# An encoder trunk with three attention kinds: values as the stationary operand in column halves, gates and gated outputs feature-major

## The reference

```python
def encoder_layer(x, ...):
    h = x @ w_in                                   # 2912 columns
    (a_q, a_k, a_v, a_g, b_cq, b_ckv, b_kr, b_g, c_q, c_k, c_v, c_g) = split(h)
    oa = window_attn(a_q, a_k, a_v, sink, t5_bias) * silu(a_g)   # 8 heads, 2 key heads, +-128 tokens
    ob = mla(b_cq, b_ckv, b_kr, ...) * silu(b_g)                 # 4 heads, all positions, rotary part
    oc = neighborhood_attn(c_q, c_k, c_v, rpb) * silu(c_g)       # 4 heads, 8x16 window of a 64-wide grid
    o = concatenate([oa, ob, oc]) @ w_out          # 512 + 256 + 256 rows
    return layer_norm(alpha * x + o)
```

## Time and profile before

| | |
|---|---|
| median of 3 runs | 2085.67 us (2085.27 to 2086.95) |
| the profiled execution, first to last instruction | 2085.9 us |
| outside that span | the span is as long as the runs' time, so nothing to add |
| mean granted TensorE clock | 0.979 of full speed |
| PE busy | 1942.8 us (93%) in 13746 instructions |
| PEld busy | 1712.9 us (82%) |
| DVE, ACT, POOL busy | 950.3 (46%), 815.9 (39%), 440.2 us (21%) |
| waits of DVE for products (line 990, 1147, 1001) | 160.0, 142.1, 68.3 us |
| first layer: input, A, C, prologue, B, output of the long sequence | 386 to 640, to 727, to 776, to 815, to 948, to 1054 us |

### The profile page before, as it was taken

The page is one execution under the profiler, slowest core; times in us unless marked ns, Lnnn a source line. Parts: engine busy times, 40 slices in busy tenths (PEclk is TensorE's granted clock), DMA queues, the critical chain, the costliest instruction groups (busy, mean ns, idle before and its releaser), DMA issues.

```text
span 2085.9 us, 35268 instructions
## 1 busy us (share of the span) xinstructions
PE 1942.8 (93%) x13746; PEld 1712.9 (82%) x13746; DVE 950.3 (46%) x2266; ACT 815.9 (39%) x1883; POOL 440.2 (21%) x476
## 2 busy tenths in 40 slices
PE   1899999999999999999959999989999999999996
PEld 0699778789998875999948986888899977689896
DVE  7335654511245655444442455452124366544436
ACT  3334652412225565443123356341231365644412
POOL 4322311410020152001132213122101114400013
PEclk9999999999999999999979999999999999999998
DMA  6455314321127010005044460422212341000312
GB/s 250 128 195 159 74 48 145 101 61 41 41 77 177 12 47 1 1 1 176 28 129 153 141 165 12 156 77 81 61 41 64 105 107 58 1 1 1 122 62 82
DMA packets 143083, 176.23 MB, mean 84 GB/s; under 512 B 18576, under 2 KB 128784, under 8 KB 142400
## 3 DMA queue, kind: packets, MB, share of 16 engines
q1 hardware_dynamic: 140976, 167.54, 26.2%
q10 hardware_dynamic: 1504, 4.78, 0.6%
q0 software_dynamic: 432, 1.57, 0.2%
HBM read 148.63 MB, written 35.80 MB: 88 GB/s over the span
## 4 chain that ended last, share of the span: by engine, by line
PE 88%; DVE 5%; ACT 3%; issue 1%; DMA 1%; POOL 1%; SPq 0%; ACTq 0%; DVEq 0%; POOLq 0%
PE psum L528 59%; PE psum L651 14%; PE psum L625 8%; PE psum L600 5%; DVE x_lo L981 2%; PE psum L538 1%; DVE hT L931 1%; ACT pAC L782 1%; DMA qkC<-ln_in_b 0%; DVE qB_lo L1123 0%; POOL w_lo L421 0%; PE psum L607 0%; PE psum L510 0%; ACT qB_hi L889 0%; ACT w_hi L814 0%
## 5 line engine op out<-in xcount | busy, mean ns | idle before, releaser
L528 PE MATMUL psum<-w_hi,x_hi 128*128 128x256 f32 x2112 | 594.5, 281 | 12.0 <-issue 7.7
L528 PE MATMUL psum<-w_lo,x_hi 128*128 128x256 f32 x2112 | 591.9, 280 | 0.0
L528 PE MATMUL psum<-w_hi,x_lo 128*128 128x256 f32 x2112 | 591.5, 280 | 0.0
L528 PEld LDWEIGHTS psum<-w_hi,x_hi 128*128 128x128 f32 x2112 | 399.2, 189 | 13.3 <-issue 13.2
L528 PEld LDWEIGHTS psum<-w_hi,x_lo 128*128 128x128 f32 x2112 | 399.0, 189 | 0.0
L528 PEld LDWEIGHTS psum<-w_lo,x_hi 128*128 128x128 f32 x2112 | 398.0, 188 | 0.2
L421 POOL TENSOR_TENSOR w_lo<-w_stage,w_hi 128x1024 fp32r<-128x1024 f32 (+1 forms) x74 | 156.7, 2123 | 743.3 <-ACT w_hi L814 743.3
L421 DVE TENSOR_TENSOR w_lo<-w_stage,w_hi 128x1024 fp32r<-128x1024 f32 (+1 forms) x70 | 140.3, 2014 | 283.4 <-ACT w_hi L814 283.4
L814 ACT ACTIVATE w_hi<-w_stage 128x1024 fp32r<-128x1024 f32 (+1 forms) x144 | 127.6, 938 | 236.1 <-PE psum L528 209.7
L790 ACT ACTIVATE pt_sb<-psum 128x256 f32<-128x256 f32 (+2 forms) x224 | 113.2, 505 | 258.8 <-PE psum L625 258.2
L1207 POOL TENSOR_TENSOR hT<-hT,rinv 128x256 f32<-128x256 f32 x96 | 58.8, 612 | 686.0 <-DVE rinv L1022 686.0
(11 more groups left out here) (140 smaller groups left out, 2925.6 us busy)
## 6 DMA issues: line engine op xcount, KB each, us to landing
w_stage<-w_in SPq DMA_DIRECT2D x72, 512.0 KB, 4.5
w_stage<-w_out SPq DMA_DIRECT2D x32, 512.0 KB, 3.9
toep<-rpb_tile SPq DMA_DIRECT2D x12, 1152.0 KB, 13.2
hT<-y SPq DMA_DIRECT2D x24, 512.0 KB, 4.7
y<-hT SPq DMA_DIRECT2D x24, 512.0 KB, 2.6
w_stage<-w_in SPq DMA_DIRECT2D x40, 256.0 KB, 3.3
rpb_tile<-rpb_col SPq DMA_DIRECT2D x48, 192.0 KB
qA<-y SPq DMA_DIRECT2D x18, 512.0 KB, 5.3
```

What stands on the lines that cost most here:

```text
L528: last = nc.tensor.matmul(out, w, x, start=(n == 0), stop=(n == len(pairs) - 1))
```

## The change

The gates become feature units (`ag0`, `ag1`, `bg`, `cg`): weights stationary, 512 tokens streaming, output feature-major in a new tile gT, in which ACT and DVE make silu 512 columns at a time. The token units shrink from seven to three (`ta`, `tb`, `tc`), and hT from 1760 to 736 columns. In the value products the values are stationary (128 x 64) and the 128 transposed probabilities stream; the two units of a pair write PSUM partitions 0 to 63 and 64 to 127, so the outputs are feature-major. The sums' reciprocals are token-major, so POOL spreads them to 64 columns each (`spread_rinv`), TensorE transposes two 128 x 128 blocks of them a group behind the value products, and DVE multiplies first these (`group_scale`), then the value products (`group_out`) into gT. gT is what the output projection needs; ACT and DVE split it directly, 1024 columns a tile, with no transposes. C's gates need no trip through memory. TensorE's order in B goes by pairs now: scores of unit 2j, first halves of the transposes of the pair before, scores of 2j + 1, second halves (long sequence only), values of the pair before.

```diff
-H_AG, H_BG, H_CG, H_AV, H_BT, H_CV = 0, 512, 768, 1024, 1152, 1504
-H_W = 1760
+H_AV, H_BT, H_CV = 0, 128, 480
+H_W = 736
 BT_KV, BT_KR = Q_RANK, Q_RANK + KV_RANK
...
+IN_UNITS = ("ck", "aq0", "aq1", "ak", "cq", "ta", "tb", "tc", "ag0", "ag1", "bg", "cg")
 UNITS = IN_UNITS + ("o0", "o1", "o2", "o3")
...
+GATE_UNITS = {"ag0": 0, "ag1": 2, "bg": 4, "cg": 6}
+FIRST_COL = {"ck": WI_CK, "cq": WI_CQ, "ak": WI_AK, "tb": WI_BT + P, "tc": WI_CV, "bg": WI_BG, "cg": WI_CG}
+TWO_PIECES = {"aq0": (WI_AQ, WI_AQ + 256), "aq1": (WI_AQ + P, WI_AQ + P + 256), "ta": (WI_AV, WI_BT),
+              "ag0": (WI_AG, WI_AG + 256), "ag1": (WI_AG + P, WI_AG + P + 256)}
...
-    n = len(units_of(ph, s))
-    pair = 1 if ph == "B" else 2
-    lags = (("S", 0), ("T", 2), ("V", 3)) if ph == "B" else (("S", 0), ("T", 1), ("V", 2))
-    steps = [(kind, pair * (j - lag) + k) for j in range(n // pair + lags[-1][1]) for kind, lag in lags
-             for k in range(pair) if 0 <= j - lag < n // pair]
+    n = len(units_of(ph, s)) // 2
+    steps = []
+    if ph == "B":
+        for j in range(n + 1):
+            if j < n:
+                steps.append(("S", 2 * j))
+            if j:
+                steps.append(("T", j - 1, 0))
+            if j < n:
+                steps.append(("S", 2 * j + 1))
+            if j:
+                if s:
+                    steps.append(("T", j - 1, 1))
+                steps.append(("V", j - 1))
+        return steps
+    for j in range(n + 2):
+        if j < n:
+            steps += [("S", 2 * j), ("S", 2 * j + 1)]
+        if 0 <= j - 1 < n:
+            steps.append(("T", j - 1, 0))
+        if 0 <= j - 2 < n:
+            steps.append(("V", j - 2))
     if ph in FILLERS:
-        steps.insert(steps.index(("T", 0)), ("fill", 0))
+        steps.insert(steps.index(("T", 0, 0)), ("fill", 0))
     return steps
...
-LAG_T, LAG_FIN = 2, 5
+LAG_T, LAG_FIN = 2, 6
...
+        gT = sb("gT", [P, KC, TMAX])
+        hflat = sb("hT", [P, NTMAX * H_W])
+        hT = hflat[:, :].rearrange("p (t n) -> p t n", t=NTMAX)
...
+            u = units_of(ph, s)[4 * g]
             if ph == "B":
-                return hT[:, g, H_BG:H_BG + 256].rearrange("p (q k n) -> p q k n", q=2, k=2)
-            u = units_of(ph, s)[4 * g]
+                return gT[:, 4:6, q_tile(g)]
             if ph == "A":
                 _, qt, _, t = u
-                return hT[:, qt:qt + 2, H_AG:H_AG + 512].rearrange("p q (k n) -> p q k n", k=2)[:, :, :, 64 * t:64 * t + 64]
+                return gT[:, t, P * qt:P * qt + 2 * P].rearrange("p (q n) -> p q n", q=2)
             _, h, w = u
-            return hT[:, w:w + 2, H_CG + 64 * h:H_CG + 64 * h + 128].rearrange("p q (k n) -> p q k n", k=2)
...
+            rb, b = divmod(w, 4)
+            rows = gT[:, 6 + h // 2, 512 * rb:512 * rb + 512].rearrange("p (r w c) -> p w r c", w=4, c=16)
...
+        def z_place(t):
...
+            return hflat[:, DM * t:DM * t + DM] if t < Z_IN_H else gT[:, t, :]
...
-            def transpose_probs(s, i, u):
-                pe.wait_ge(probs_done, probs_no[s, u])
-                src = pB[:, i % 3, :] if u[0] == "B" else pAC[:, i % 3, :]
-                for hf, chunks in enumerate(halves_of(u, s)):
+            def transpose_probs(s, ph, j, hf):
+                for i in (2 * j, 2 * j + 1):
+                    u = units_of(ph, s)[i]
+                    pe.wait_ge(probs_done, probs_no[s, u])
+                    src = pB[:, i % 3, :] if ph == "B" else pAC[:, i % 3, :]
...
-                    for c in chunks:
...
-            def values(s, i, u):
...
+                return vB[:, c, 64 * u[2]:64 * u[2] + 64]
...
+            def values(s, ph, j):
...
+                okey = ("O", s, ph, j // 2)
                 b = uses[okey][0]
-                if i % 4 == 0:
+                if j % 2 == 0:
                     wait_free(pe, okey)
-                    if i == 4 and u[0] in FILLERS:
-                        wait_full(pe, ("fill", s, u[0]))
-                out = bank[b][:, 64 * (i % 4):64 * (i % 4) + 64]
-                nk = key_tiles(u, s)
-                for hf, chunks in enumerate(halves_of(u, s)):
...
-                    wait_copied(s, (u, hf))
-                    slot = half_index[s, (u, hf)] % 4
+                    if j == 2 and ph in FILLERS:
+                        wait_full(pe, ("fill", s, ph))
+                pair = units_of(ph, s)[2 * j:2 * j + 2]
+                nk = key_tiles(pair[0], s)
+                cols = slice(P * (j % 2), P * (j % 2) + P)
+                for hf, chunks in enumerate(halves_of(pair[0], s)):
+                    for u in pair:
+                        wait_copied(s, (u, hf))
                     for c in chunks:
-                        if u[0] == "A":
-                            _, qt, kv, t = u
-                            v = hT[:, max(qt - 1, 0) + c, H_AV + 64 * kv:H_AV + 64 * kv + 64]
-                        elif u[0] == "C":
-                            _, h, w_ = u
-                            rb, wb = divmod(w_, 4)
-                            v = vwin[:, wb * (SEQ_LEN[s] // 256) + rb + c, 64 * h:64 * h + 64]
-                        else:
-                            v = vB[:, c, 64 * u[2]:64 * u[2] + 64]
-                        last = nc.tensor.matmul(out, pt_sb[:, slot, (c % 4) * P:(c % 4 + 1) * P], v,
-                                                start=(c == 0), stop=(c == nk - 1))
-                if i % 4 == 3:
+                        for k, u in enumerate(pair):
+                            slot = half_index[s, (u, hf)] % 4
+                            nc.tensor.matmul(bank[b][64 * k:64 * k + 64, cols], value_tile(s, u, c),
+                                             pt_sb[:, slot, (c % 4) * P:(c % 4 + 1) * P], start=(c == 0), stop=(c == nk - 1))
+                if j % 2:
+                    g = j // 2
+                    pe.wait_ge(rinv_spread, group_no[s, ph, g])
+                    for m in range(2):
+                        last = nc.tensor.transpose(bank[b][:, 256 + P * m:256 + P * m + P], rinv_wide[:, P * m:P * m + P], ident[:, :])
                     last.then_inc(bank_full[b], 1)
...
-                        for kind, i in pe_steps(ph, s):
+                        for kind, i, *hf in pe_steps(ph, s):
                             if kind == "fill":
                                 keep_warm(s, ph)
+                            elif kind == "S":
+                                score(s, i, U[i])
+                            elif kind == "T":
+                                transpose_probs(s, ph, i, hf[0])
                             else:
-                                {"S": score, "T": transpose_probs, "V": values}[kind](s, i, U[i])
...
-                        wait_read(pe, ("O", s, "B", len(b_units(s)) // 4 - 1 - g))
-                    for t in range(4):
-                        transposes(s, "oT", t)
...
-                        if n == 0 and t % 4 == 0:
-                            wait_parts(s, "oT", t)
-                        if n == 0 and t in (0, 2) and NT > 4:
-                            transposes(s, "oT", t + 4)
-                            transposes(s, "oT", t + 5)
+                        if n == 0:
...
-                        if u not in TOKEN_UNITS:
+                        if u in GATE_UNITS:
+                            for c, j in feature_order(s, u):
+                                key = (u, s, j, c)
+                                ps = wait_full(act, key)
+                                g = gate_no[s, u, c, j]
+                                if g > 2:
+                                    act.wait_ge(silu_done, g - 2)
+                                nc.scalar.activation(tanh_g[:, (g - 1) % 2, :], ps, ACT.Tanh, scale=0.5)
+                                nc.scalar.activation(gT[:, GATE_UNITS[u] + j, 512 * c:512 * (c + 1)], ps, ACT.Copy,
+                                                     scale=0.5).then_inc(free(key), 1)
+                        elif u not in TOKEN_UNITS:
                             if u == "cq" and s:
...
-                                pt_copy(s, U[i - LAG_T])
+                                if ph == "B" and s:
+                                    for u in U[i // 2 * 2 - 2:i // 2 * 2]:
+                                        pt_copy(s, u, i % 2)
+                                else:
+                                    pt_copy(s, U[i - LAG_T], 0)
                             if i < len(U):
...
+                        wait_read(act, ("O", s, "B", len(b_units(s)) // 4 - 1 - g))
                     for t in range(NT):
-                        high_part("oT", s, t)
+                        nc.scalar.activation(x_hi[:, :, q_tile(t)], gT[:, :, q_tile(t)], ACT.Copy).then_inc(o_hi_done, 1)
                     split_high(s, NU - 3)
...
                     split_high(s, NU - 1)
-                    norm_steps(layer_ln, [hT[:, t, 0:DM] for t in range(NT - 1)], ln_no[s, 0] - 1)
...
+            def sub_tiles(ps, ph, at):
...
```

(56 more changed lines are left out.)

279 lines of the change are left out of this document (128 added, 151 removed).

## The result

The changed kernel takes 2022.49 us (median of 4 runs, 2020.98 to 2023.28) against 2085.78 of the kernel before on the same chip: ratio 0.9699, 95% interval 0.9688 to 0.9711, 63 us less. The forecast was 1990, 96 less. The span of the profiled execution, from its first to its last instruction, is 2020.2 us against 2085.9, so 65.7 us are to be found.

What follows compares the result with a forecast made beforehand. TensorE matmuls were taken to carry the chain of waits. Per layer -28.2 - 17.4 + 7.5 - 2.1 - 13.2 + 5 = -48.4, twice -96.8 from 2085.9 us: forecast 1990 us, range 1960 to 2050.

Steps and rivals of the forecast that it cites:

- Value products: Phases A and C: pairs of column halves at 0.118 us; with the added reciprocal transposes, -28.2 us a layer.
- the zero for the changes of layout: Value blocks: going between full width and column halves costs nothing; paid at both ends it would be +40 us.
- Rival 1: Value products: each instruction pays its load, 0.16 us a pair; -23.8 us a layer, 2038 us; chance 0.12.
- Rival 2: Value products: loads unhidden or pair one after the other, 0.21 to 0.236 us; 2108 to 2145 us; chance 0.13.
- Rival 3: A and C: DVE last, steps not under 2.7 us; B short's idles lower the clock; 2025 us; chance 0.12.
- B, long: Phase B, long sequence: a pair takes 7.03 us against 8.12, with 0.31 idle; -17.4 us a layer.
- B, short: Phase B, short sequence: a pair takes 5.00 us against 4.06, waiting for DVE's copy; +7.5 us a layer.
- fill: Phase ends and B's start and end: one more DVE product, later first transposes, last copies; +5 us a layer.
- Into the output projection: Last value product to first output product: 3.7 us, without transposes; -4.1 short and -9.1 long, -13.2 us a layer.
- Gates: Gate products: 1152 instructions 256 wide become 576 that are 512 wide; 136.5 against 134.4 us, -2.1 a layer.

## Why the prediction was right, and where its sum was off

The direction, the range (1960 to 2050) and the mechanism held; 31 us of the 97 in the sum were not there. By its own steps:

**Value products: the pair was right, the zero for the changes of layout was not.** I took 0.118 us a pair; it is 0.109. I took nothing for going between full width and column halves, from the latent transposes, where single 64-column transposes stand among full ones at 0.11. That reading of the rows was right, but they were not a case of the change that counts here; no run shows why. For the value blocks it is 0.10 on the way in (transposes 0.71 to 0.81) and 0.04 more than before on the way out, and 0.15 more on the reciprocals' pair, which has such a way out behind it. A and C per layer, 72 blocks and 36 groups: pairs 384 x (0.109 - 0.118) = -3.5, in 7.2, out 2.9, reciprocals 36 x 0.15 = 5.4 (the last three are 15.5; the 104 changes at 0.15 each are 15.6): 12.0 us more than forecast. Forecast -28.2, measured -15.5: the miss is 12.7, and this names nearly all of it, 24 to 25 us of the two layers. The run with the reciprocals ahead in A and C shows that it is the change and not the instruction: 0.15 us a group go away when one such change is taken out and nothing else. The same changes stand in B, in smaller number; what they cost there was not taken apart. The Trainium skill (TensorEngine Tiling (Array Packing), Key Properties) says that a change of tiling mode drains TensorE; I had its price as +40 us over all blocks. What is measured, 0.14 us for each of the blocks in A and C, agrees with it in that a change costs time, and is about two thirds of 2 x 0.105; the emptying itself is not in the trace.

**Rival 1, loads not hidden**, fell. It asked for 0.16 us a pair. The load instructions of the value products last 0.137 us each, and two a pair are hidden in 0.109. The Trainium skill (TensorE: Matmul & The Clock Gate, Part 3) lets loads overlap running products only where the row groups differ; here both halves use all rows and the trace does not agree.

**Rival 2, no gain from the halves**, fell by 0.109 a pair, and the run with both units in one half shows what it would have cost: 1.46 us a block and 2099 us, 9 under the low end of its 2108 to 2145, with B still on two halves.

**Rival 3, DVE last in A and C**, fell: steps of 2.46 us and no idle. Its other half, the clock brought down by the idles of B short, fell too: 1.00 over 34 us of such pairs. The slow stretch at B's start (0.50 from 272 to 278 us) stands behind the prologue, as in the kernel before. The run with values before transposes shows how thin the cover is.

**B, long.** Forecast 7.03 us a pair with an idle of 0.31, measured 7.11 with 0.17: right. **B, short.** Forecast 5.00 a pair with an idle of 1.6 ended by DVE's copy, measured 5.02 and 5.20 with 1.47: right in place, cause and size, and the run with the copy first shows the cause. With fill: B per layer -7.7 and -7.5, forecast -9.9 and some +3.

**Into the output projection.** Forecast 3.7 us from the last value product, measured 3.96. The forecast gain of 13.2 a layer counted the 16 transposes behind the first product of the long sequence, 1.76 us, as part of the wait. With them the measured gains are 12.3 and 12.0 a layer (10.6 and 10.2 by the table's cut), so the wait itself lacks only 2.1 us in all. What the sum lacked is what comes next, the slow start at half the clock: in the long sequence 26 output instructions are 0.213 instead of 0.118 us apart, 2.5 us a place, which the transposes bore before. Over the four places the slow starts behind the first output product cost 9.0 us now and 3.3 before, so 5.7 more.

**Gates.** Forecast -2.1 a layer. The products did shrink, but the spacing of the old ones was 0.118 rather than 0.1185, which leaves some 0.6 to 1.3 us, and the first scores of A now wait for the eviction of the last gates:

```profile
194.91 1.35 PE L635 MATMUL psum<-kA,qA 64*128 64x256 f32 x8 [1.27 <-ACT gT L876]
```

1.27 us where it was 0.84, and 0.54 in the long sequence where there was none. Net nothing. The stretches from the first output product to the next A changed by -0.6 and +3.8 us, where the forecast had -4.2 for the gates and, by this cut, -3.5 for the transposes: 10.9 us, of which the slow starts are 5.7 and the gates, with these waits, most of the rest. No run changed the gates alone, so what is theirs in this is read from the trace and not shown.

Summed over both layers, measured less forecast: A and C +25.5, entries +2.1, output and gates +10.9, B and fill -5.4 (fill +10 was in the forecast, and B has -15.2 against -19.8), start -1.3. That is 32, for the 31 between 96.8 and 65.7.

## What to carry to other kernels

Price a change of TensorE's layout where blocks are short: 0.14 us is a sixth of a block of 12 instructions, and whatever full-width work there is belongs beside other full-width work. A queue in order makes a wait out of a position: the copy that TensorE needed next stood behind a reduction that nothing needed yet, and the swap gave 19 us for no work at all. And a wait made shorter gives back less than its length if the engine leaves it at half its clock (here up to 2.6 us a place), or if it then only waits longer for the next weights (3.17 us for 1.92).

## What the runs showed of the hardware

- Two products of 64 stationary columns in different halves of the columns, with all 128 rows each, start within 0.01 us of each other and stream 128 float32 columns together in 0.109 us; two in the same half take 0.218.
- A product for the idle half overtakes queued products of the busy half: by the starts, the seventh instruction in the queue started 0.275 us after the first, 0.10 before the fourth (one unit first, block at 735.9). Which row of starts is which half is inferred from their spacing. I had expected starts in the order of the queue.
- Each change between full width, row halves and column halves costs 0.15 us, 0.094 at the change and 0.05 to 0.06 before the second instruction or pair behind it; one 64-column transpose among full-width ones costs nothing that the trace shows.
- After the same idle of 3.5 us the granted clock was 0.50 for the next 12 to 27 output instructions, and in two places (reciprocals ahead in all phases, long sequence) for none; with products of the identity in that idle it stayed at 1.00 in all four places.
